# Gate and up products of a dense feed-forward by seven half-size products instead of eight

## The chip, the core and the metric

The program runs on one core of a Trainium2 chip. TensorE (PE in the profile) multiplies matrices into PSUM, VectorE (DVE) and ScalarE (ACT) work element by element, GpSimd (POOL) and SyncE (SP) here mostly start DMA transfers. Each engine runs its own instruction stream, and the streams meet at semaphores. The metric is the device time of one launch in microseconds (us); lower is better.

## What is computed

Two transformer stacks of two layers each run on one sequence of 256 tokens of 1024 values, all in float32. What matters here are three dense feed-forward blocks (both layers of the first stack, the first layer of the second), each of width 2816:

```python
gate, up = jnp.split(jnp.einsum('bsd,df->bsf', h, ffn_w_gate_up[l]), 2, axis=-1)
f = jnp.einsum('bsf,fd->bsd', jax.nn.silu(gate) * up, ffn_w_down[l])

def dense_swiglu(x, w_gate, w_up, w_down):
    return (jax.nn.silu(x @ w_gate) * (x @ w_up)) @ w_down
```

The last layer has a mixture of eight experts of width 3584 instead, which takes the time from about 1450 us to the end. The change does not touch it.

## The kernel before

**Stages.** The program is a list of stages (mixers, projections, norms, feed-forwards), and each engine walks the same list with its own code. Weights are read from memory once, in blocks of at most 2 MB, into six slots of SBUF (`slots`); SP starts the load of block n as soon as TensorE has marked block n - 6 as used. So a load follows TensorE's progress.

**One dense feed-forward.** The 2816 columns are cut into six groups: five of 512 and one of 256. A group has a gate block, an up block (1024 x 512) and a down block (512 x 1024). The tokens lie transposed in `hT`: 128 partitions x 8 chunks of the 1024 input values x 256 tokens. A *pair* is 256 columns of a group, so a group of 512 has two pairs, the last group one. A pair has two *units*, gate and up: 256 output columns x 256 tokens x 1024 inputs. The first group (`first_gate_up`) is worked in halves of 128 tokens, since the two token tiles become ready one after the other; the other five groups go through `gate_up`: 9 pairs, 18 units in each feed-forward, 54 units in the program.

**One unit before.** For each of two blocks of 128 columns, TensorE adds up eight products over the chunks k in one PSUM bank (128 x 512: two blocks x 256 tokens):

```python
last = pe.matmul(b[:, f * S:(f + 1) * S], v[:, k, (f0 + f) * P:(f0 + f + 1) * P],
                 hT[:, k, :], start=(k == 0), stop=(k == KD - 1))
```

The weights' 128 x 128 block is the operand that is loaded into the array (LDWEIGHTS), the 256 tokens are moved through it. Gate units go to the two banks `ps_a`, up units to the two banks `ps_d`. ScalarE takes silu of the gate bank into `silu`, VectorE multiplies that with the up bank into `hid` (part of the buffer `proj`).

**Order on TensorE.** Group 0 (halves), gate and up of group 1, down of group 0, gate and up of group 2, down of group 1, and so on; the downs of the last two groups come after the last gate and up, one token tile after the other. `down` (16 products of 512 moved columns for a full group) accumulates in the four banks `ps_s` and `ps_x` and waits for `hid` of its own pairs only.

Of the kernel before, what the change touches and what calls it, by code (L numbers as in the profile page):

```python
# [25 lines left out]
P = 128  # L26
D = 1024
S = 256
# [471 lines left out]
def build(nc, a, out, book, cut=None):  # L500
# [21 lines left out]
    with ExitStack() as ctx:  # L522
        def sb(name, shape, dt=F32):
            return ctx.enter_context(nc.sbuf_tensor(name, shape, dt))
# [5 lines left out]
        def sem(name):  # L530
# [19 lines left out]
        dve_order, act_order, pool_order, exped, maxed = (  # L550
            sem(n) for n in ("dve_order", "act_order", "pool_order", "exped", "maxed"))

        slots = sb("slots", [P, SLOTS, SLOT])
        X = sb("X", [P, T, D])
        N = sb("N", [P, T, D])
# [56 lines left out]
        order_s = flat[:, 3200:3456]  # L612
        earlier, every = QK[:, 0, 0, :], QK[:, 0, 1, :]
        silu = flat[:, 2048:3072].rearrange("p (b s) -> p b s", b=2)
        logits = flat[:, 3072:3088].rearrange("p (t e) -> p t e", t=T)
        route = flat[:, 3088:3200]
        NF = N[:, :, :].rearrange("p t c -> p (t c)")
        VC = NF[:, 0:1024].rearrange("p (t c) -> p t c", t=T)
        score = NF[:, 1024:1536].rearrange("p (t s) -> p t s", t=T)
        work = NF[:, 1536:2048].rearrange("p (t s) -> p t s", t=T)  # L620
        DOf = DO[:, :, :].rearrange("p t c -> p (t c)")
# [357 lines left out]
        def _(pe):  # L979
# [246 lines left out]
            def first_gate_up(group, s, stage_n):  # L1226
# [18 lines left out]
                state["pair"] += group["w"] // P // 2  # L1245
                return state["pair"] - 1

            def gate_up(group):
                gv, uv = slot(group["gate"]), slot(group["up"])
                for f0 in range(0, group["w"] // P, 2):  # L1250
                    for w, v, r in (("gate", gv, "a"), ("up", uv, "d")):
# [8 lines left out]
                group_pair = state["pair"] - 1  # L1260
                return group_pair
# [499 lines left out]
        def _(act):  # L1761
# [146 lines left out]
            def ffn(s, stage_n):  # L1908
                for t in range(T):
                    turn_tile(s, stage_n, t)  # L1910
                for group in s["groups"]:
                    for _ in range(group["w"] // P // 2):
                        b, n = bank(lane, "a")
                        act.wait_ge(*lane.of(("full", "a", n)))
                        p = state["pair"]
                        state["pair"] += 1
# [229 lines left out]
        def _(dve):  # L2146
# [609 lines left out]
            def ffn(groups):  # L2756
                for group in groups:
                    n_group = state["group"]
                    state["group"] += 1
                    dve.wait_ge(*lane.back(("down",), n_group - 2))  # L2760
                    for f0 in range(0, group["w"] // P, 2):
                        p = state["pair"]
                        state["pair"] += 1
                        dve.wait_ge(*lane.of(("silu", p)))
                        b, n = bank(lane, "d")
                        dve.wait_ge(*lane.of(("full", "d", n)))
                        dve.tensor_tensor(  # L2767
                            hid[:, n_group % 2, f0:f0 + 2, :].rearrange("p f s -> p (f s)"), silu[:, p % 2, :],
                            b[:, :], ALU.mult).then_inc(*lane.tick(d_free, ("free", "d", n), ("hidden", p)))

            for n, (kind, s) in enumerate(stages):
                lane.ring.update(ring_at[n])
# [4 lines left out]
                if kind == "lines":  # L2777
                    b, m = bank(lane, "d")
                    dve.wait_ge(*lane.of(("full", "d", m)))
                    for v in range(2):  # L2780
                        do(dve.tensor_tensor(lines[:, v, :], b[0:16, :], line_mask[:, v, :], ALU.add),
                           ("lines",), ("free", "d", m), sem=d_free)
                elif kind == "norm":
                    norm(s, n)
                elif kind == "last_norm":
                    last_norm(s)
                elif kind == "first_slots":
                    first_slots(s["steps"], s["downs"])
                elif kind == "head_norms":
                    head_norms(s)  # L2790
                elif kind == "mla_keys":
                    mla_keys()
                elif kind == "attend":
                    attend(s, n)
                elif kind == "attend_head":
                    attend(stages[n + s["ahead"]][1], n + s["ahead"], head=True)
                elif kind == "latent_norm":
                    dve.wait_ge(*lane.of(("latent",)))
                    dve.wait_ge(*lane.of(("lin", s["src"], 0, 1)))
                    c = proj[:, :, 512:640]  # L2800
                    squares(c, P, SQ[:, 0])
                    inv_root(T, stat[:, 32:34], 1.0 / P, LN_EPS)
                    for t in range(T):
                        do(dve.scalar_tensor_tensor(c[:, t, :], c[:, t, :], stat[:, t:t + 1], small[:, 0:P],
                                                    ALU.mult, ALU.mult), ("latent_normed",))
                elif kind == "index_scores":
                    do(dve.memset(score, 0.0))
                    dve.wait_ge(*lane.of(("lin", s["src"], 1, 1)))
                    do(dve.tensor_scalar(proj[:, :, 1216:1224], proj[:, :, 1216:1224], 8 ** -0.5, None, ALU.mult))
                    for h in range(8):  # L2810
                        dve.wait_ge(*lane.of(("relu", h)))
                        for t in range(T):
                            do(dve.scalar_tensor_tensor(score[:, t, :], PR[h // 2 % 2][:, h % 2, t, :],
                                                        proj[:, t, 1216 + h:1217 + h], score[:, t, :],
                                                        ALU.mult, ALU.add), ("indexed", h))
                elif kind == "select":
                    select(s)
                elif kind == "gates":
                    dve.wait_ge(*lane.of(("gate_exp",)))
                    do(dve.tensor_scalar(gate_t[:, :, :], gate_t[:, :, :], 1.0, None, ALU.add))  # L2820
                    do(dve.reciprocal(gate_t[:, :, :], gate_t[:, :, :]))
                elif kind == "compress_in":
                    compress_in()
                elif kind == "compress_hidden":
                    compress_hidden()
                elif kind == "compress_out":
                    compress_out()
                elif kind == "ended_scores":
                    ended_scores()
                elif kind == "ended_out":  # L2830
                    ended_out(n)
                elif kind == "latent_heads":
                    attend(stages[n + 1][1], n + 1, head=True)
                elif kind == "route":
                    route_tokens(s)
                elif kind == "ffn":
                    ffn(s["groups"])
# [40 lines left out]
```

## Time and profile before

| | us |
|---|---|
| median of 3 runs | 2364.01 |
| lowest and highest | 2359.44 and 2368.95 |
| the profiled execution | 2360.85 |
| its span, first to last instruction | 2359.0 |
| TensorE busy | 2260.9 |
| VectorE busy | 451.3 |
| ScalarE busy | 354.3 |

The span and the profiled execution's own time lie 1.85 us apart; the profiled execution lies 3.16 us under the median. The profile records each float32 matmul as two passes, each with a weight load and a product: `gate_up` issues 27 pairs x 16 = 432 products into `ps_a`, and line 1256 has 864 of them. A product's record lasts longer than its share of the engine, because products overlap; the distance from start to start is what one costs.

### The profile page before, as it was taken

The page shows a single profiled execution, that of the slowest core. Times are in us where ns is not written, and L with a number is a line of the kernel's source. Part 1 is how long each engine was busy: PE and PEld are TensorE (multiplying, and loading weights), DVE is VectorE, ACT ScalarE, POOL GpSimd, SP SyncE. Part 2 cuts the span into 40 slices and gives each one's busy share as a digit, 9 for nine tenths or more (in the row PEclk, how much of TensorE's full clock was granted, in tenths as well). Part 3 has the DMA queues.
Part 4 walks back from the last instruction along what each step waited for, and adds up shares of the span by engine and source line. Part 5 has one row for each costly group of instructions (what it writes and reads, how often), then busy time and mean ns, then how long its engine had stood idle before and what let it go on. Part 6 is the DMA issues. An engine that isn't in the chain of part 4 may idle for free. (4 is left out here: it accounts for less than half of the span.)

```text
span 2359.0 us, 31883 instructions
## 1 busy us (share of the span) xinstructions
PE 2260.9 (96%) x13831; PEld 1331.0 (56%) x13831; DVE 451.3 (19%) x1173; ACT 354.3 (15%) x891; POOL 108.0 (5%) x188
## 2 busy tenths in 40 slices
PE   8999999999999999999999998999899899989986
PEld 5769675687777567787758766333333233323322
DVE  3231002342000344200021534101010011101012
ACT  1330000161000123200001613110010011000000
POOL 2202000001000011000000200000000000000000
PEclk9799999999999999999998998999999999999998
DMA  9605424584444353444343434899999999999994
GB/s 305 216 17 205 166 85 163 149 196 165 150 143 138 100 199 141 152 160 143 104 149 134 149 116 160 341 368 406 407 405 409 404 409 404 409 400 409 400 409 183
DMA packets 196934, 564.32 MB, mean 239 GB/s; under 512 B 9832, under 2 KB 25384, under 8 KB 196792
## 3 DMA queue, kind: packets, MB, share of 16 engines
q1 hardware_dynamic: 187352, 536.95, 61.3%
q0 software_dynamic: 9440, 25.28, 3.7%
q8 instruction: 113, 1.85, 0.3%
q14 instruction: 29, 0.24, 0.0%
HBM read 554.60 MB, written 7.60 MB: 238 GB/s over the span
## 5 line engine op out<-in xcount | busy, mean ns | idle before, releaser
L1256 PE MATMUL ps_a<-hT,slots 128*128 128x256 f32 x864 | 190.9, 379 | 0.0
L1256 PE MATMUL ps_d<-hT,slots 128*128 128x256 f32 x864 | 190.9, 379 | 0.0
L1505 PE MATMUL ps_d<-slots,hT 128*32 128x512 f32 x1456 | 183.2, 593 | 6.9 <-DMA late<-in_moe_w_up 2.6
L1256 PEld LDWEIGHTS ps_a<-hT,slots 128*128 128x128 f32 x864 | 163.9, 190 | 27.3 <-issue 5.7
L1256 PEld LDWEIGHTS ps_d<-hT,slots 128*128 128x128 f32 x864 | 164.2, 190 | 22.3
L1505 PE MATMUL ps_d<-slots,N 128*32 128x512 f32 x1344 | 166.3, 593 | 8.1 <-DMA slots<-in_moe_w_up 3.0
L1054 PE MATMUL ps_a<-hT,slots 128*128 128x256 f32 (+1 forms) x768 | 144.3, 349 | 1.9 <-ACT hT L1791 1.5
L1054 PEld LDWEIGHTS ps_a<-hT,slots 128*128 128x128 f32 x768 | 127.4, 193 | 19.1 <-issue 5.6
L2767 DVE TENSOR_TENSOR proj<-proj,ps_d 128x512 f32<-128x512 f32 x33 | 22.7, 687 | 590.6 <-PE ps_d L1256 519.3
L2690 DVE TENSOR_TENSOR proj<-proj,ps_d 64x512 f32<-64x512 f32 (+2 forms) x32 | 22.1, 689 | 569.9 <-PE ps_d L1505 321.0
L1273 PE MATMUL ps_x<-slots,proj 128*128 128x512 f32 x264 | 121.6, 592 | 0.0
L1273 PE MATMUL ps_s<-slots,proj 128*128 128x512 f32 x264 | 121.6, 592 | 0.0
L1505 PEld LDWEIGHTS ps_d<-slots,hT 128*32 128x32 f32 x1456 | 51.9, 110 | 118.0 <-issue 114.0
L1029 PE MATMUL ps_a<-slots,hT 128*128 128x512 f32 (+5 forms) x320 | 107.1, 491 | 2.8 <-ACT hT L1791 2.8
L1505 PEld LDWEIGHTS ps_d<-slots,N 128*32 128x32 f32 x1344 | 47.1, 110 | 108.6 <-issue 103.6
L1918 ACT ACTIVATE proj<-ps_a 128x512 f32<-128x512 f32 x33 | 19.7, 597 | 537.7 <-PE ps_a L1256 511.6
L1572 PE MATMUL ps_x<-slots,PT 128*32 128x512 f32 x672 | 80.0, 621 | 16.1 <-DMA slots<-in_moe_w_down 15.3
L1989 ACT ACTIVATE PT<-ps_a 128x512 f32<-128x512 f32 x44 | 25.1, 596 | 423.6 <-PE ps_a L1594 423.5
L1553 PE MATMUL ps_x<-slots,PT 128*32 128x512 f32 x672 | 88.4, 593 | 0.0
L1029 PEld LDWEIGHTS ps_a<-slots,hT 128*128 128x128 f32 x320 | 59.5, 199 | 47.8 <-issue 45.2
L1273 PEld LDWEIGHTS ps_x<-slots,proj 128*128 128x128 f32 x264 | 50.2, 190 | 63.1 <-issue 63.1
L1273 PEld LDWEIGHTS ps_s<-slots,proj 128*128 128x128 f32 x264 | 50.2, 190 | 56.7 <-issue 56.0
(403 smaller groups left out, 2587.7 us busy)
## 6 DMA issues: line engine op xcount, KB each, us to landing
slots<-in_moe_w_gate SPq DMA_DIRECT2D x43, 2048.0 KB, 20.6
slots<-in_moe_w_down SPq DMA_DIRECT2D x42, 2048.0 KB, 20.9
slots<-in_moe_w_up SPq DMA_DIRECT2D x41, 2048.0 KB, 23.0
slots<-in_ffn_w_gate_up SPq DMA_DIRECT2D x20, 2048.0 KB, 8.0
late<-in_moe_w_up SPq DMA_DIRECT2D x15, 2048.0 KB, 23.0
late<-in_moe_w_down SPq DMA_DIRECT2D x14, 2048.0 KB, 20.4
late<-in_moe_w_gate SPq DMA_DIRECT2D x13, 2048.0 KB, 23.9
slots<-in_ffn_w_down SPq DMA_DIRECT2D x10, 2048.0 KB, 8.1
```

Source lines behind the costliest of these rows:

```text
L1029: last = pe.matmul(b[:, 0:c], lhs[:, k, t * P:(t + 1) * P], v[:, k, :], start=(k == 0), stop=(k == s["k"] - 1))
L1054: last = pe.matmul(b[:, f * S + tokens.start:f * S + tokens.stop], v[:, k, part["c"] + P * f:part["c"] + P * f + P], lhs[:, k, tokens], st ...
L1256: last = pe.matmul(b[:, f * S:(f + 1) * S], v[:, k, (f0 + f) * P:(f0 + f + 1) * P], hT[:, k, :], start=(k == 0), stop=(k == KD - 1))
L1273: last = pe.matmul(b[:, :], hid[:, n_group % 2, f, t * P:(t + 1) * P], v[:, f, half * 512:(half + 1) * 512], start=start, stop=stop)
L1505: last = pe.matmul(b[TILE * j:TILE * j + TILE, :], x[:, k, TILE * c:TILE * c + TILE], views[w][:, k % deep, 512 * h:512 * h + 512], start= ...
L1553: last = pe.matmul(b0[TILE * j:TILE * j + TILE, :], mine(f + o, c), v[:, f + o, 512 * half:512 * half + 512], start=(first and o == 0), st ...
L1572: last = pe.matmul(b[TILE * j:TILE * j + TILE, :], hid_a[:, f, o:o + TILE], v[:, f, 512 * half:512 * half + 512], start=(at == 0 and f == ...
L1918: act.activation(silu[:, p % 2, :], b[:, :], ACT.Silu).then_inc(*lane.tick(a_free, ("free", "a", n), ("silu", p)))
L1989: act.activation(dst.rearrange("p f s -> p (f s)"), b[:, :], ACT.Copy).then_inc(*lane.tick(a_free, ("free", "a", n), *[("hid_turned", i) f ...
L2690: post(dve.tensor_tensor(hidden[low:high, half, :], gated[low:high, half, :], b[low:high, :], ALU.mult), *marks, *([("free", r, n)] if m = ...
L2767: dve.tensor_tensor(hid[:, n_group % 2, f0:f0 + 2, :].rearrange("p f s -> p (f s)"), silu[:, p % 2, :], b[:, :], ALU.mult).then_inc(*lane. ...
```

## The change

All groups but the first go by Strassen's scheme (in the variant with common sums). A unit is seen as a 2 x 2 block product: inputs in two halves (chunks 0 to 3 and 4 to 7), columns in two blocks of 128 (f0, f0 + 1), tokens in two tiles of 128. Instead of eight half-size products there are seven, each of four chunks, of 128 columns x 128 tokens.

- **TensorE** (`gate_up`, `seven_products`): a unit takes two banks of its ring. The first gets three products, the second four; each product adds up four chunks. Before a unit it waits for `weights_summed`.
- **VectorE before the products**: once in a feed-forward `sum_tokens` makes four sums of token quarters (128 x 512 each) into the buffers `PR`; for each unit `sum_weights` makes four sums of weight quarters (128 x 512 each), three into a buffer for gate (`PT`) or up (part of `proj`), one in place in the weight slot. There is one such buffer each for gate and up. Sums for group 1 are made ahead of the first multiply of group 0.
- **After the products**: ScalarE copies one 128 x 128 product to SBUF; VectorE's `join` adds them up in four instructions (256, 256, 256 and 128 values per partition) into SBUF (`N`). ScalarE then takes silu from there, VectorE multiplies from there.
- **VectorE's order in the loop**: join gate of pair p, sums of gate weights of p + 1, join up of p, sums of up weights of p + 1, multiply p.

```diff
             def gate_up(group):
-                        b, n = bank(lane, r)
-                        pe.wait_ge(*emptied(lane, r, n))
-                        for f in range(2):
-                            for k in range(KD):
-                                last = pe.matmul(b[:, f * S:(f + 1) * S], v[:, k, (f0 + f) * P:(f0 + f + 1) * P],
-                                                 hT[:, k, :], start=(k == 0), stop=(k == KD - 1))
-                        last.then_inc(*lane.tick(filled[r], ("full", r, n), ("used", group[w])))
+                        v, (t2, t3, t4) = views[w], weight_sums[w]
+                        b11, t1 = (v[:, 0:4, P * f:P * f + P] for f in (f0, f0 + 1))
+                        b21, b22 = (v[:, 4:8, P * f:P * f + P] for f in (f0, f0 + 1))
+                        b, n = bank(lane, r)
+                        pe.wait_ge(*emptied(lane, r, n))
+                        pe.wait_ge(*lane.of(("weights_summed", w, state["pair"])))
+                        seven_products([(0, b11, a11), (1, b21, a12), (2, t2, s2)], b, n, r)
+                        b, n = bank(lane, r)
+                        pe.wait_ge(*emptied(lane, r, n))
+                        seven_products([(2, t3, s3), (1, t1, s1), (0, t4, a22), (3, b22, s4)], b, n, r, ("used", group[w]))
...
+            def seven_products(products, b, n, r, *keys):
+                for at, lhs, rhs in products:
+                    for k in range(4):
+                        last = pe.matmul(b[:, P * at:P * at + P], lhs[:, k, :], rhs[:, k, :], start=(k == 0), stop=(k == 3))
+                last.then_inc(*lane.tick(filled[r], ("full", r, n), *keys))
...
+            def sum_weights(w, group, f0, p):
+                dve.wait_ge(*lane.of(("weights", group[w])))
+                do(dve.tensor_tensor(t3, b22, b12, ALU.subtract), sem=weights_summed)
+                do(dve.tensor_tensor(b12, b12, b11, ALU.subtract), sem=weights_summed)
+                do(dve.tensor_tensor(t2, b22, b12, ALU.subtract), sem=weights_summed)
+                do(dve.tensor_tensor(t4, b21, t2, ALU.subtract), ("weights_summed", w, p), sem=weights_summed)
...
+            def join(w, r, p):
+                dve.wait_ge(*lane.of(("first", w, p)))
+                do(dve.tensor_tensor(ahead_of[w].rearrange("p (m s) -> p m s", m=2)[:, :, 0:P],
+                                     one.unsqueeze(1).broadcast_to([P, 2, P]),
+                                     first[:, P:3 * P].rearrange("p (m s) -> p m s", m=2), ALU.add), ("free", r, n), sem=joined)
+                dve.wait_ge(*lane.of(("full", r, n)))
+                do(dve.tensor_tensor(u[:, 1:3], u[:, 0:1].broadcast_to([P, 2, P]), m[:, 1:3], ALU.add), sem=joined)
+                do(dve.tensor_tensor(c[:, :, 1], u[:, 2:3].broadcast_to([P, 2, P]), m[:, 0:2], ALU.add), sem=joined)
+                do(dve.tensor_tensor(c[:, 1, 0], u[:, 1], m[:, 3], ALU.add), ("free", r, n), ("joined", w, p), sem=joined)
```

TensorE, first feed-forward, from the end of group 0 on, before: one pair is a gate unit and an up unit of 16 products with 256 moved columns each; after two pairs the down of group 0 follows.

```order
L1240 MATMUL ps_d<-hT,slots 128x128 x16
L1256 MATMUL ps_a<-hT,slots 128x256 [waits a_free,slot_landed0,slot_landed5]
L1256 MATMUL ps_a<-hT,slots 128x256 x15
L1256 MATMUL ps_d<-hT,slots 128x256 [waits d_free]
L1256 MATMUL ps_d<-hT,slots 128x256 x15
```

The same place after (`PR` and `late` hold token sums, `PT` and `proj` weight sums); the rows are one gate unit and the head of its up unit.

```order
L1251 MATMUL ps_d<-hT,slots 128x128 x16
L1263 MATMUL ps_a<-hT,slots 128x128 [waits a_free,weights_summed,slot_landed0,slot_landed5]
L1263 MATMUL ps_a<-hT,slots 128x128 x7
L1263 MATMUL ps_a<-PR,PT 128x128 x4
L1263 MATMUL ps_a<-late,PT 128x128 [waits a_free]
L1263 MATMUL ps_a<-late,PT 128x128 x3
L1263 MATMUL ps_a<-PR,slots 128x128 x4
L1263 MATMUL ps_a<-hT,PT 128x128 x4
L1263 MATMUL ps_a<-late,slots 128x128 x4
L1263 MATMUL ps_d<-hT,slots 128x128 [waits weights_summed,d_free]
L1263 MATMUL ps_d<-hT,slots 128x128 x7
```

A unit of 16 products of 256 columns became 28 products of 128 columns, with a wait for VectorE at its head and a wait for its second bank after 12 products.

VectorE in the same feed-forward, before: one multiply for each pair is all that it does there.

```order
L2767 TENSOR_TENSOR proj<-proj,ps_d 128x512 [waits d_full,a_free,x_landed0]
L2767 TENSOR_TENSOR proj<-proj,ps_d 128x512 [waits d_full,a_free]
L2767 TENSOR_TENSOR proj<-proj,ps_d 128x512 [waits d_full,a_free,down_done]
L2767 TENSOR_TENSOR proj<-proj,ps_d 128x512 [waits d_full,a_free]
L2767 TENSOR_TENSOR proj<-proj,ps_d 128x512 [waits d_full,a_free,down_done]
```

VectorE after, for the first pair of group 1: the join of gate, the sums for the next pair's gate, and the join of up.

```order
L2820 TENSOR_TENSOR N<-N,ps_a 128x2x128 [waits act_order]
L2826 TENSOR_TENSOR N<-N,ps_a 128x256 [waits a_full,joined]
L2827 TENSOR_TENSOR N<-N,ps_a 128x2x128 [waits joined]
L2828 TENSOR_TENSOR N<-N,ps_a 128x128 [waits joined]
L2809 TENSOR_TENSOR PT<-slots 128x512 [waits slot_landed5,joined]
L2810 TENSOR_TENSOR slots<-slots 128x4x128 [waits weights_summed]
L2811 TENSOR_TENSOR PT<-slots 128x512 [waits weights_summed]
L2812 TENSOR_TENSOR PT<-slots,PT 128x512 [waits weights_summed]
L2820 TENSOR_TENSOR N<-proj,ps_d 128x2x128 [waits act_order,weights_summed]
L2826 TENSOR_TENSOR N<-N,ps_d 128x256 [waits d_full,joined]
L2827 TENSOR_TENSOR N<-N,ps_d 128x2x128 [waits joined]
L2828 TENSOR_TENSOR N<-N,ps_d 128x128 [waits joined]
```

Behind these follow four sums for the next pair's up and the multiply of this pair; where one instruction stood for a pair, 17 stand now, and the sums for the next gate unit stand behind the last three joins of this one.

## Rows read from the trace of the kernel before

**Rows 1.** The page: busy time by engine, then the span in 40 slices.

```profile
PE 2260.9 (96%) x13831; PEld 1331.0 (56%) x13831; DVE 451.3 (19%) x1173; ACT 354.3 (15%) x891; POOL 108.0 (5%) x188
...
PE   8999999999999999999999998999899899989986
...
PEclk9799999999999999999998998999999999999998
DMA  9605424584444353444343434899999999999994
```

**Rows 2.** Windows: first group, gate and up, down, experts; busy time of each engine.

```profile
core 0: us, PE busy (x) PEld busy (x) DVE busy (x) ACT busy (x) POOL busy (x), PEclk, DMA share, GB/s
176.80:206.86 30.06, 29.79 (x264) 29.57 (x265) 6.58 (x12) 4.29 (x8) 15.26 (x21) 1.00 0.64 213
206.86:234.49 27.63, 27.63 (x130) 24.33 (x129) 1.37 (x2) 1.19 (x2) 0.00 (x0) 1.00 0.53 200
234.49:248.23 13.74, 13.74 (x34) 6.08 (x33) 0.69 (x1) 0.00 (x0) 0.00 (x0) 1.00 0.47 165
1450.00:2350.00 900.00, 845.77 (x7199) 288.26 (x7197) 108.03 (x216) 83.57 (x148) 0.53 (x1) 0.97 0.97 384
```

**Rows 3.** Timeline of PE, first feed-forward: group 0 second half, group 1, down.

```profile
start us, us, engine line op out<-in xcount [idle before <-releaser]
192.47 3.84 PE L1240 MATMUL ps_a<-hT,slots 128*128 128x128 f32 x32 [0.25 <-ACT hT L1791]
196.14 3.74 PE L1240 MATMUL ps_d<-hT,slots 128*128 128x128 f32 x32
199.72 3.74 PE L1240 MATMUL ps_a<-hT,slots 128*128 128x128 f32 x32
203.29 3.74 PE L1240 MATMUL ps_d<-hT,slots 128*128 128x128 f32 x32
206.86 7.07 PE L1256 MATMUL ps_a<-hT,slots 128*128 128x256 f32 x32
213.77 7.07 PE L1256 MATMUL ps_d<-hT,slots 128*128 128x256 f32 x32
...
234.49 1.88 PE L1273 MATMUL ps_s<-slots,proj 128*128 128x512 f32 x4
...
248.23 2.11 PE L1256 MATMUL ps_a<-hT,slots 128*128 128x256 f32 x9
```

**Rows 4.** Instructions of line 1240 and line 1256: duration in ns, least, median, greatest.

```profile
L1240 PEld LDWEIGHTS ps_a<-hT,slots x384: 186/192/192, 176.8 to 1019.7; 128*128 128x128 f32 x192
L1256 PE MATMUL ps_a<-hT,slots x864: 379/379/382, 206.9 to 1195.7; 128*128 128x256 f32 x173
```

**Rows 5.** Line 1239: what a wait beyond an instruction's own becomes on PE's queue.

```profile
L1239 PEldq EVENT_SEMAPHORE  x3: 51/51/51, 176.7 to 993.4; - x3
```

**Rows 6.** Groups by line and shape on DVE and ACT: count, busy us, mean ns.

```profile
L2767 DVE TENSOR_TENSOR proj<-proj,ps_d 128x512 f32<-128x512 f32 x33 | 22.7, 687 | 590.6 <-PE ps_d L1256 519.3 <-PE ps_d L1240 71.3
L2209 DVE TENSOR_TENSOR X<-X,N 128x1024 f32<-128x1024 f32 x8 | 9.8, 1224 | 0.3
L2390 DVE TENSOR_TENSOR hT<-hT 128x256 f32<-128x256 f32 x8 | 3.4, 425 | 0.3
L2343 DVE TENSOR_TENSOR late<-late,N 128x128 f32<-128x128 f32 x6 | 1.7, 285 | 0.0
L1861 ACT ACTIVATE late<-ps_s,negmax 128x128 f32<-128x128 f32 x24 | 9.3, 387 | 0.2
```

**Rows 7.** Timeline of DVE and ACT in the first feed-forward.

```profile
191.82 1.08 ACT L1791 ACTIVATE hT<-ps_s 128x512 f32<-128x512 f32 x2 [9.83 <-PE ps_s L1007]
...
234.76 0.69 DVE L2767 TENSOR_TENSOR proj<-proj,ps_d 128x512 f32<-128x512 f32 x1 [13.10 <-PE ps_d L1256]
...
400.05 1.23 DVE L2209 TENSOR_TENSOR X<-X,N 128x1024 f32<-128x1024 f32 x1
401.31 1.22 DVE L2211 CUSTOM_DVE_ANT_0 N<-X 128x1024 f32<-128x1024 f32 x1
```

**Rows 8.** What SP waits for before it starts loads, then one load and its landing time.

```profile
SPq L790 <- PE ps_a L1256: 263.6, 15, 20.3
...
SPq L790 <- PE ps_d L1505: 207.4, 51, 18.0
...
slots<-in_ffn_w_gate_up SPq DMA_DIRECT2D x20, 2048.0 KB, 8.0
```

**Rows 9.** Timeline of SP: the loads of groups 3 (gate, up) and 2 (down).

```profile
227.78 7.27 SPq L790 DMA_DIRECT2D slots<-in_ffn_w_gate_up  x2
248.42 0.37 SPq L790 DMA_DIRECT2D slots<-in_ffn_w_down  x1
```

More of the change, by code:

```diff
@@ L614, in build @@
         silu = flat[:, 2048:3072].rearrange("p (b s) -> p b s", b=2)
+        token_sums = [buf.rearrange("p a t s -> p (a t s)")[:, 512 * i:512 * i + 512].rearrange("p (k s) -> p k s", k=4)
+                      for buf in (PR[0][:, :, :, :], PR[1]) for i in range(2)]
+        weight_sums = {w: [buf[:, 512 * i:512 * i + 512].rearrange("p (k c) -> p k c", k=4) for i in range(3)]
+                       for w, buf in (("gate", PT[:, :, :, :, :].rearrange("p a j k n -> p (a j k n)")[:, 0:1536]),
+                                      ("up", flat[:, 3072:4608]))}
         logits = flat[:, 3072:3088].rearrange("p (t e) -> p t e", t=T)
@@ L618, in build @@
         VC = NF[:, 0:1024].rearrange("p (t c) -> p t c", t=T)
+        whole = {"gate": NF[:, 0:512], "up": NF[:, 512:1024]}
+        partial = NF[:, 1024:1408].rearrange("p (m s) -> p m s", m=3)
+        ahead_of = {"gate": NF[:, 0:2048], "up": NF[:, 512:1536]}
+        first_product = {"gate": NF[:, 1408:1536], "up": flat[:, 4608:4736]}
         score = NF[:, 1024:1536].rearrange("p (t s) -> p t s", t=T)
@@ L1910, in ffn @@
                     turn_tile(s, stage_n, t)
-                for group in s["groups"]:
+                for g, group in enumerate(s["groups"]):
                     for _ in range(group["w"] // P // 2):
+                        p = state["pair"]
+                        state["pair"] += 1
+                        if not g:
+                            bank(lane, "d")
+                        if g:
+                            for w, r in (("gate", "a"), ("up", "d")):
+                                b, n = bank(lane, r)
+                                bank(lane, r)
+                                act.wait_ge(*lane.of(("full", r, n)))
+                                act.activation(first_product[w], b[:, 0:P], ACT.Copy).then_inc(*lane.tick(act_order, ("first", w, p)))
+                            act.wait_ge(*lane.of(("joined", "gate", p)))
+                            act.wait_ge(*lane.back(("hidden",), p - 2))
+                            act.activation(silu[:, p % 2, :], whole["gate"], ACT.Silu).then_inc(*lane.tick(act_order, ("silu", p)))
+                            continue
                         b, n = bank(lane, "a")
                         act.wait_ge(*lane.of(("full", "a", n)))
-                        p = state["pair"]
-                        state["pair"] += 1
                         act.wait_ge(*lane.back(("hidden",), p - 2))
@@ L2754, in expert, with sum_tokens @@
                             *lane.tick(emptying[r], ("free", r, n)))
[L2756 to L2759, printed above, removed]
-                    dve.wait_ge(*lane.back(("down",), n_group - 2))
[L2761 to L2769, printed above, removed]
+            def sum_tokens(stage_n):
+                for t in range(T):
+                    dve.wait_ge(*lane.of(("hT", stage_n, t, 4)))
+                a11, a12 = hT[:, 0:4, 0:P], hT[:, 4:8, 0:P]
+                a21, a22 = hT[:, 0:4, P:S], hT[:, 4:8, P:S]
+                s1, s2, s3, s4 = token_sums
+                do(dve.tensor_tensor(s1, a21, a22, ALU.add), sem=tokens_summed)
+                do(dve.tensor_tensor(s2, s1, a11, ALU.subtract), sem=tokens_summed)
+                do(dve.tensor_tensor(s3, a11, a21, ALU.subtract), sem=tokens_summed)
+                do(dve.tensor_tensor(s4, a12, s2, ALU.subtract), sem=tokens_summed)
@@ new lines, in ffn @@
+            def ffn(groups, stage_n):
+                sum_tokens(stage_n)
+                units = [(group, f0) for group in groups for f0 in range(0, group["w"] // P, 2)]
+                lead, p0 = groups[0]["w"] // P // 2, state["pair"]
+                for w in ("gate", "up"):
+                    sum_weights(w, *units[lead], p0 + lead)
+                for _ in range(lead):
+                    bank(lane, "a")
+                for i, (group, f0) in enumerate(units):
+                    p = p0 + i
+                    if f0 == 0:
+                        n_group = state["group"]
+                        state["group"] += 1
+                    target = hid[:, n_group % 2, f0:f0 + 2, :].rearrange("p f s -> p (f s)")
+                    if i >= lead:
+                        for w, r in (("gate", "a"), ("up", "d")):
+                            join(w, r, p)
+                            if i + 1 < len(units):
+                                sum_weights(w, *units[i + 1], p + 1)
+                    dve.wait_ge(*lane.back(("down",), n_group - 2))
+                    dve.wait_ge(*lane.of(("silu", p)))
+                    if i >= lead:
+                        dve.tensor_tensor(target, silu[:, p % 2, :], whole["up"], ALU.mult).then_inc(
+                            *lane.tick(dve_order, ("hidden", p)))
+                        continue
+                    b, n = bank(lane, "d")
+                    dve.wait_ge(*lane.of(("full", "d", n)))
+                    dve.tensor_tensor(target, silu[:, p % 2, :], b[:, :], ALU.mult).then_inc(
+                        *lane.tick(d_free, ("free", "d", n), ("hidden", p)))
+                state["pair"] += len(units)
@@ L2836, in _ @@
                 elif kind == "ffn":
-                    ffn(s["groups"])
+                    ffn(s["groups"], n)
                 elif kind == "experts":
```

18 lines of the change are left out of this document (14 added, 4 removed).

## The prediction

> **What bounds the kernel now.** I read the page's busy line and slices first [rows 1]. TensorE is busy 96% of the span, VectorE 19%, ScalarE 15%. The DMA row falls into two parts: some four tenths up to slice 23, nine tenths after it. So TensorE's work sets the time before the experts, and transfers may set it there. Next the windows [rows 2]: in the gate and up window of group 1 TensorE is busy for all of 27.63 us, VectorE for 1.37 us, DMA for 0.53 of the time; in the experts DMA is at 0.97. The feed-forwards are therefore TensorE's, without a gap to fill. Then the timeline [rows 3], for what one product costs. Its second number is the length of the records of a group; the first numbers, the starts, give the rate. Last come VectorE's groups and gaps [rows 6, 7], because it gets the new work, and SP's waits [rows 8, 9], because a gain on TensorE counts only if the loads behind it move as well.
>
> **The change part by part: TensorE.** Four units of group 1 run from 206.86 to 234.49 us [rows 3], so a unit takes 27.63 / 4 = 6.908 us. It has 16 products of two passes each (864 records for 432 products, [rows 4]); a pass of 256 columns thus costs 6.908 / 32 = 215.9 ns. A new unit has 28 products of 128 columns, 56 passes. The columns moved fall to 7/8 (56 x 128 against 32 x 256), but the weight loads rise from 32 to 56. What a pass of 128 columns with a fresh 128 x 128 load costs needn't be guessed: group 0 consists of such passes. From 196.14 to 206.86 us there are 96, without a gap [rows 3]: 111.7 ns each, only 3.7 ns above half a 256-column pass. A load's record lasts 192 ns [rows 4], yet starts follow at 111.7 ns, so loads overlap their neighbours; the load rows fill 29.57 of 30.06 us there [rows 2], so hardly any room is left. New unit: 56 x 111.7 = 6.253 us. Gain: 0.654 us a unit, in 54 units **35.3 us**. The granted clock was 1.00 (the 2.4 GHz level) in both windows [rows 2], and the new stream is as dense, so I leave it there.
>
> The Trainium skill speaks against this step: "TensorE: Matmul & The Clock Gate", section "Back-to-back issue gap", gives a stream of load and product pairs some 81 ns per product at 128 columns, where the columns alone would take about 56, that is 1.46 times as much. Applied as a ratio, an estimate from that page, a pass here would cost 158 ns and a unit 8.8 us, and the kernel would end near 2468 us. The trace has 1.03 times instead [rows 3], and that decides.
>
> **Waits on TensorE.** A unit's head now has one wait more, and in its middle one for the second bank. A wait beyond an instruction's own became an instruction of 51 ns on PE's queue [rows 5]. Down's first product waits for more than one thing too (four in the first feed-forward), and yet starts 27.63 us after the units, in step with 32 passes each [rows 3]: no cost there, but behind slow passes. In a stream of 111.7 ns passes the queue has less time to hide it. Bounds: 0 and 54 x 0.051 = 2.8 us; a further wait can't make a pass quicker, so nothing below nought. Neither row is nearer; I take the middle, 1.4 us.
>
> **VectorE, sums.** No row shows a sum of 512 values out of SBUF alone. An addition of 512 with one operand in PSUM takes 687 ns, one of 1024 within SBUF 1224 ns [rows 6], which halved is 612. I take 687, since the fixed part of a short instruction is in it; the far end is 1224. From start to start 30 ns come on top (400.05 to 401.31 against 1.224, [rows 7]). A unit's four sums: 4 x 0.717 = 2.87 us. The joins: 256 values take 425 ns, 128 take 285 ns [rows 6]; 3 x 0.455 + 0.315 = 1.68 us. Together 4.55 us a unit beside 6.25 us of TensorE, and over 54 units, with the 12 token sums, some 254 us more busy time on VectorE, all of it off the path as long as each deadline holds.
>
> **The deadline.** There is one weight-sum buffer each for gate and up, so the sums of the next gate unit may begin only when this one has ended, and so for up. From a unit's end: 0.27 us until VectorE starts (234.76 against 234.49, [rows 3, 7]), the last three joins 1.23 us, the sums 2.87 us: ready 4.37 us after. TensorE spends 6.25 us on the other unit meanwhile: **1.9 us to spare**. Behind the last pair of a group a down of 13.74 us lies between as well [rows 2]. The join's first instruction needs ScalarE's copy of 128 values (nearest row 387 ns, [rows 6]) of a bank filled 3.5 us before the unit ends, so it is done by then. What is queued behind these waits on VectorE is the multiply; down needs it only after the next group's units.
>
> **Start and end of a feed-forward.** VectorE can begin its token sums when `hT` is copied, at 192.90 us [rows 7]. Four sums and the four for gate end at 198.6; TensorE wants them at 206.86. The first multiply waits behind all 12, to 201.5 us; its bank is wanted at 213. At the end the last pair is ready 0.27 + 1.23 + 0.72 = 2.2 us after its unit, while TensorE first does half of a down, 13.74 / 2 = 6.9 us [rows 2]. Nothing is exposed; if the cover failed, this costs at most a few us in each of three feed-forwards.
>
> **Loads.** VectorE asks for a group's weights about 20 us sooner than TensorE did. Group 3's gate and up were issued from 227.78 us on [rows 9] and land after some 8 us [rows 8]; VectorE asks for them in the second pair of group 2, after 260 us. SP waits for TensorE's marks in the feed-forwards and in the experts alike [rows 8], so the stages behind, the DMA-bound one too, start earlier by the whole gain.
>
> **The sum.** Against the profiled execution: 2360.85 - 35.3 + 1.4 = 2326.9 us. That execution lies 3.2 us under the median of the runs, so **2330 us**.
>
> **The rivals.**
>
> *VectorE late* (slower). For: the sums are strided over four chunks, read two SBUF operands, and depend on each other; such a shape isn't in the trace. Against: additions within SBUF cost what their length says [rows 6]. Only the second pair of each two-pair group is exposed, 24 units (2 units x 4 groups x 3). Were all the instructions twice as long, a unit's sums would be ready after 0.27 + 2 x 4.10 = 8.5 us, 2.2 us late: 24 x 2.2 = 53 us lost on top of the forecast, 2330 + 53 = **2383 us**. It decides from 1.80 times the rows' durations on (0.27 + 1.80 x 4.10 = 7.65 us, 1.4 us late, x 24 = 34 us). Chance 0.06.
>
> *Weight loads not hidden* (slower). If loads from the sum buffers don't overlap as group 0's do, a pass costs up to its load's 192 ns [rows 4]: 56 x 0.192 = 10.75 us a unit, 3.84 us more, 207 us in all: 2571 us. It decides from 6.908 / 56 = 123.4 ns a pass on, which makes the margin thin: 10% above group 0's. Against: same form, same stream, 96 passes in a row at 111.7. Chance 0.04. By the page above this rival would end at 2468.
>
> *Half of it lost*. Each wait that VectorE or a bank releases late by 0.1 to 0.3 us over 54 units takes 5 to 16 us: 2335 to 2346 us. Chance 0.09.
>
> *No change*. Some 0.45 us or more of stall a unit, or a later stage that waits for something else than TensorE. Against the latter: SP's waits [rows 8]. Around 2358 us. Chance 0.05. That fewer products are issued than seven, or more, the order of the instructions excludes.
>
> **How the numbers follow.** The forecast has 0.76, at 2330 us; with its own bounds (0 or 2.8 us of waits, and runs that spread by 5 us either way) 2323 to 2337. To hold 8 in 10 the range takes in most of the half-lost case: 2321 to 2346. Faster by over 0.5% (about what a measurement of this kernel can tell from no change, 12 us): 0.76 + 0.09 = 0.85; within it 0.05; slower 0.06 + 0.04 = 0.10.
>
> **What would show it.** In the profile after: units 6.25 us apart from start to start, 56 passes each of 111 to 112 ns, load rows nearly without a gap; group 1 with its down in 38.8 us instead of 41.4; VectorE's sums at 0.69 us and its busy time near 705 us; no idle time of TensorE ahead of the units put down to VectorE; the experts as long as before, only earlier. Wrong would be: TensorE waiting for the sums at the second pair's units, passes above 123 ns, or sums well over 1 us.

## The result and the profile after

| | before | after |
|---|---|---|
| median, us | 2363.82 (4 runs) | 2327.25 (4 runs) |
| lowest and highest, us | 2359.44 and 2368.95 | 2323.76 and 2330.76 |
| the profiled execution, us | 2360.85 | 2323.76 |
| its span, us | 2359.0 | 2322.0 |

The ratio of the times is 0.9845, 95% interval 0.9829 to 0.9861: the changed kernel is faster by 36.6 us of the medians. The forecast was 2330 us, with a range of 2321 to 2346.

The page's busy line of the kernel after, to be held against [rows 1]:

```profile
PE 2226.2 (96%) x15127; PEld 1338.5 (58%) x15127; DVE 694.9 (30%) x1617; ACT 367.2 (16%) x945; POOL 108.5 (5%) x188
```

TensorE is busy 34.7 us less, VectorE 243.6 us more, and the span fell by 37.0 us. VectorE's work has thus left no mark that can be seen from this far. Next the windows of the kernel after. The columns are those of [rows 2]; the first line is group 1's gate and up, the second the down of group 0, the third both together, the last a stretch of the experts.

```profile
206.06:231.07 25.01, 25.01 (x226) 25.01 (x225) 14.66 (x27) 2.15 (x6) 0.00 (x0) 1.00 0.56 211
231.07:244.81 13.74, 13.74 (x35) 6.09 (x34) 4.59 (x8) 0.00 (x0) 0.00 (x0) 1.00 0.52 181
206.06:244.81 38.75, 38.75 (x259) 31.10 (x258) 19.25 (x35) 2.15 (x6) 0.00 (x0) 1.00 0.55 200
1413.00:2313.00 900.00, 846.61 (x7197) 287.49 (x7195) 107.75 (x215) 83.62 (x148) 0.53 (x1) 0.97 0.98 384
```

Gate and up of a group take 25.01 us where they took 27.63, the down 13.74 as before. TensorE is still busy for the whole window, and so now is its weight load (25.01 of 25.01). VectorE is busy for 14.66 us of it instead of 1.37, and the clock stays at 1.00. A 900 us stretch of the experts holds nearly the same work at the same DMA share, begun 37 us earlier. The experts' first product shows the same shift, 37.5 us, before (first line) and after (second line):

```profile
1471.78 8.79 PE L1505 MATMUL ps_d<-slots,hT 128*32 128x512 f32 x80 [0.50 <-ACT hT L1926]
1434.29 13.94 PE L1528 MATMUL ps_d<-slots,hT 128*32 128x512 f32 x128 [0.50 <-ACT hT L1961]
```

(The two counts and lengths differ because the listings end at different times.)

The timeline of TensorE after shows the same group from start to start; the columns are those of [rows 3]. The lines left out are the other products of each unit.

```profile
206.06 1.95 PE L1263 MATMUL ps_a<-hT,slots 128*128 128x128 f32 x16
207.84 1.06 PE L1263 MATMUL ps_a<-PR,PT 128*128 128x128 f32 x8
...
211.42 1.06 PE L1263 MATMUL ps_a<-late,slots 128*128 128x128 f32 x8
212.31 1.95 PE L1263 MATMUL ps_d<-hT,slots 128*128 128x128 f32 x16
...
218.56 1.95 PE L1263 MATMUL ps_a<-hT,slots 128*128 128x128 f32 x16
...
224.82 1.95 PE L1263 MATMUL ps_d<-hT,slots 128*128 128x128 f32 x16
...
231.07 1.88 PE L1296 MATMUL ps_s<-slots,proj 128*128 128x512 f32 x4
```

Units start at 206.06, 212.31, 218.56 and 224.82 us, and the down at 231.07: 25.01 / 4 = 6.25 us a unit, 56 passes of 111.7 ns. No line of these four units carries an idle time in brackets, the lines left out included, so TensorE waited neither for sums nor for a bank.

How the sums fit beside this is seen on VectorE, from the end of the gate unit of the first pair (212.31 us) on:

```profile
212.58 0.42 DVE L2826 TENSOR_TENSOR N<-N,ps_a 128x256 f32<-128x256 f32 x1 [2.91 <-PE ps_a L1263]
213.04 0.42 DVE L2827 TENSOR_TENSOR N<-N,ps_a 128x256 f32<-128x256 f32 x1
213.49 0.29 DVE L2828 TENSOR_TENSOR N<-N,ps_a 128x128 f32<-128x128 f32 x1
213.81 0.69 DVE L2809 TENSOR_TENSOR PT<-slots 128x512 f32<-128x512 f32 x1
...
215.99 0.69 DVE L2812 TENSOR_TENSOR PT<-slots,PT 128x512 f32<-128x512 f32 x1
```

VectorE starts 0.27 us after the unit's end, and the last of the four sums ends at 215.99 + 0.69 = 216.68 us, 4.37 us after it. TensorE wants them at 218.56.

**Where the time went.** I measured the first and the third feed-forward from the first product of group 0 to the first transpose of the norm behind it. The second is measured from the transposes between the two token halves of group 0 on, in both kernels, so it lacks the first half of group 0, which the change doesn't touch. These are windows of the kernel before (the first three lines) and of the kernel after (the last three), one line for each feed-forward, with the same columns:

```profile
176.82:406.72 229.90, 229.65 (x1017) 172.39 (x1017) 21.63 (x37) 11.34 (x20) 15.26 (x21) 1.00 0.45 158
571.36:786.90 215.54, 215.29 (x891) 158.03 (x890) 12.93 (x21) 10.42 (x16) 0.00 (x0) 1.00 0.40 138
993.47:1223.38 229.91, 229.66 (x1017) 172.40 (x1017) 17.98 (x28) 10.97 (x18) 9.76 (x19) 1.00 0.42 143
```

```profile
176.01:394.15 218.14, 217.89 (x1448) 175.52 (x1449) 103.75 (x185) 15.63 (x38) 15.69 (x21) 1.00 0.48 167
558.71:762.49 203.78, 203.53 (x1323) 161.16 (x1322) 93.09 (x169) 14.83 (x34) 0.00 (x0) 1.00 0.42 147
969.30:1187.45 218.15, 217.90 (x1449) 175.52 (x1449) 98.16 (x176) 15.26 (x36) 9.75 (x19) 1.00 0.43 151
```

Each lost 11.76 us (229.90 - 218.14, and so on), that is 18 units x 0.653 us; three times that is 35.3 us. The remaining 1.7 us of the two spans lie outside the feed-forwards, where the change does nothing: 0.8 us ahead of the first one, 1.6 us between the third and the experts, and the rest with the other sign. They are within what two executions of one kernel differ by.

### The profile page after: what moved, and what is told of

Read it like the earlier page. It is cut to its first block, busy times and chain, and to the rows that moved or that the text cites. A ratio compares the mean times of both kernels' runs of the same rounds, so it can differ in the third digit from the quotient of the medians.

```text
span 2322.0 us, 35165 instructions
## 1 busy us (share of the span) xinstructions
PE 2226.2 (96%) x15127; PEld 1338.5 (58%) x15127; DVE 694.9 (30%) x1617; ACT 367.2 (16%) x945; POOL 108.5 (5%) x188
## 4 chain that ended last, share of the span: by engine, by line
PE 85%; DMA 10%; ACT 2%; POOL 1%; DVE 1%; SPq 1%; issue 1%; DVEq 0%; ACTq 0%
PE ps_d L1528 14%; PE ps_d L1263 7%; PE ps_a L1263 7%; PE ps_a L1065 6%; PE ps_s L1296 5%; PE ps_x L1296 5%; PE ps_a L1040 5%; PE ps_x L1576 4%; PE ps_s L1528 4%; PE ps_x L1177 3%; DMA late<-in_moe_w_up 3%; PE ps_s L1110 3%; PE ps_x L1110 3%; PE ps_x L1595 2%; DMA slots<-in_moe_w_up 2%; PE ps_x L1582 2%
## 5 line engine op out<-in xcount | busy, mean ns | idle before, releaser
L1065 PEld LDWEIGHTS ps_a<-hT,slots 128*128 128x128 f32 x768 | 127.4, 193 | 19.2 <-issue 5.6
L1528 PE MATMUL ps_d<-late,N 128*32 128x512 f32 x512 | 74.6, 593 | 2.6 <-DMA slots<-in_moe_w_up 1.5
L1110 PE MATMUL ps_s<-slots,hT 128*128 128x512 f32 x160 | 72.2, 596 | 2.7 <-ACT hT L1825 2.7
L1177 PE MATMUL ps_x<-proj,PT 128*128 128x64 f32 (+1 forms) x560 | 71.6, 284 | 0.0
L1177 PEld LDWEIGHTS ps_x<-proj,PT 128*128 128x128 f32 x560 | 70.5, 204 | 0.0
L1110 PE MATMUL ps_x<-slots,hT 128*128 128x512 f32 x160 | 69.6, 592 | 0.0
L2003 ACT ACTIVATE proj<-ps_d 32x512 f32<-32x512 f32 (+3 forms) x56 | 33.1, 591 | 222.4 <-PE ps_d L1528 221.8
```

Source lines behind the costliest of these rows:

```text
L1065: last = pe.matmul(b[:, f * S + tokens.start:f * S + tokens.stop], v[:, k, part["c"] + P * f:part["c"] + P * f + P], lhs[:, k, tokens], st ...
L1110: last = pe.matmul(b[:, :], hT[:, k, t * P:(t + 1) * P], v[:, k, :], start=(k == ks[0]), stop=(k == ks[-1]))
L1177: last = pe.matmul(b[:, o:o + dv], PT[:, u % 2, j, turned_at[kc, t], :], named[name][:, kc, c:c + dv], start=(kc == kcs[0]), stop=(kc == k ...
L1528: last = pe.matmul(b[TILE * j:TILE * j + TILE, :], x[:, k, TILE * c:TILE * c + TILE], views[w][:, k % deep, 512 * h:512 * h + 512], start= ...
L2003: act.activation(dst, src, ACT.Silu).then_inc(*lane.tick(a_free if frees else act_order, ("gate_silu", q), *([("free", "d", n)] if frees e ...
```

## The experiments

The theory: TensorE's passes are the whole of it, seven eighths of the columns at nearly the same price per column, and VectorE's sums lie in TensorE's shadow with under 2 us to spare. Against it stood that the new pass costs more than counted, that the sums or the waits cost something which another gain hides, and that the spare time is no more than a number on paper.

### The shape alone: eight products in halves

The kernel before, with each unit's 256 tokens moved in two halves of 128. All eight half-size products remain, and nothing is summed.

```diff
-                            for k in range(KD):
-                                last = pe.matmul(b[:, f * S:(f + 1) * S], v[:, k, (f0 + f) * P:(f0 + f + 1) * P],
-                                                 hT[:, k, :], start=(k == 0), stop=(k == KD - 1))
+                            for t in range(T):
+                                for k in range(KD):
+                                    last = pe.matmul(b[:, f * S + t * P:f * S + t * P + P],
+                                                     v[:, k, (f0 + f) * P:(f0 + f + 1) * P],
+                                                     hT[:, k, t * P:t * P + P], start=(k == 0), stop=(k == KD - 1))
```

> The kernel before, with each unit cut into eight half-size products (four blocks of 128 columns x 128 tokens, each over eight chunks) instead of products of 256 moved columns: the shape of the changed kernel without its seventh saved. My theory (a pass of 128 columns costs 111.7 ns wherever it stands, and only the number of passes counts): a unit takes 64 x 111.7 = 7.15 us instead of 6.91, 54 units lose 12.9 us, so 12 to 14 us above the kernel before. Rival (the gain of the change comes from its shape or from smaller products, not from their number): at or below the time before. Rival (a pass of 128 columns is dearer in some other place than group 0): over 14 us above it.

Measured: 2380.28 us median, against 2364.62 of the kernel before beside it; ratio 1.0053, interval 1.0035 to 1.0070, so 12.5 us slower (2364.62 x 0.0053). The two medians lie 15.7 us apart, which taken alone would be past the 14 us of the second rival. The window of the first feed-forward decides between them:

```profile
179.26:413.48 234.22, 233.97 (x1592) 191.59 (x1593) 21.64 (x37) 11.34 (x20) 15.25 (x21) 1.00 0.45 155
```

It takes 4.32 us more than before (234.22 - 229.90), in three feed-forwards 13.0 us, so a pass of 128 columns isn't dearer here than in group 0. The timeline of TensorE in this kernel:

```profile
209.31 7.31 PE L1257 MATMUL ps_a<-hT,slots 128*128 128x128 f32 x64
216.45 7.31 PE L1257 MATMUL ps_d<-hT,slots 128*128 128x128 f32 x64
223.60 7.31 PE L1257 MATMUL ps_a<-hT,slots 128*128 128x128 f32 x64
230.75 7.31 PE L1257 MATMUL ps_d<-hT,slots 128*128 128x128 f32 x64
237.89 1.88 PE L1275 MATMUL ps_s<-slots,proj 128*128 128x512 f32 x4
```

A unit takes (237.89 - 209.31) / 4 = 7.145 us, which is 64 passes of 111.6 ns. So the gain of 0.654 us a unit falls into two parts: the smaller blocks cost 7.145 - 6.908 = 0.24 us, and the eighth product that isn't made gives back 8 x 111.7 = 0.89 us.

### No sums at all

The kernel after, without the token sums, the weight sums and TensorE's wait for them; each product takes a plain quarter in place of the sum. Its values are thus others, and send the tokens to other experts. That makes the last stage, and the whole time, something else (4905.75 us), so only the feed-forwards compare.

```diff
-                s1, s2, s3, s4 = token_sums
+                s1, s2, s3, s4 = hT[:, 0:4, P:S], hT[:, 4:8, 0:P], hT[:, 4:8, P:S], hT[:, 0:4, 0:P]
...
+                        t2, t3, t4 = b11, b21, b22
...
-                        pe.wait_ge(*lane.of(("weights_summed", w, state["pair"])))
...
             def sum_weights(w, group, f0, p):
-                dve.wait_ge(*lane.of(("weights", group[w])))
+                return
...
-                sum_tokens(stage_n)
```

> The changed kernel without the sums of weights and of tokens and without TensorE's wait for them: the seven products take plain quarters of weights and tokens instead, so the block products are not those of the layer. The joins stay. My theory (VectorE's sums lie wholly beside TensorE's work): within 3 us of the changed kernel, 2327 us, units still 6.25 us apart. Rival (the sums or the waits for them cost TensorE something): faster by 5 us or more.

The total missed what was expected (within 3 us of the changed kernel), since I had not thought of the tokens' way to the experts. The window of the first feed-forward of this kernel, whole as above:

```profile
176.20:394.34 218.14, 217.89 (x1448) 175.59 (x1449) 49.57 (x109) 15.62 (x38) 15.27 (x21) 1.00 0.48 167
```

It takes 218.14 us, as with the sums, though VectorE is busy 49.57 us in it instead of 103.75. The third feed-forward takes 218.14 us too, against 218.15. Sums and waits for them cost TensorE nothing that a hundredth of a microsecond shows.

### How much room there is: two, three and four more sums

The kernel after, with the sum into `t2` made again two, three or four times, the result unchanged. The kernel with three more was made after the other two had been measured, and its forecast draws on them. For two more:

```diff
                 do(dve.tensor_tensor(t2, b22, b12, ALU.subtract), sem=weights_summed)
+                do(dve.tensor_tensor(t2, b22, b12, ALU.subtract), sem=weights_summed)
+                do(dve.tensor_tensor(t2, b22, b12, ALU.subtract), sem=weights_summed)
                 do(dve.tensor_tensor(t4, b21, t2, ALU.subtract), ("weights_summed", w, p), sem=weights_summed)
```

> The changed kernel with the third sum of each unit's weights made three times instead of once, two instructions of 0.72 us more before the sums are ready. My theory (1.9 us to spare between the sums and the unit that needs them): ready 5.8 us after the last unit of the same kind instead of 4.4, still ahead of 6.25, so the time stays within 3 us of the changed kernel. Rival (less is to spare than that, or VectorE's load counts by itself): 54 x 1.43 us at worst, 77 us slower; anything over 5 us speaks for it.

> As the kernels with two and with four more, with three instructions of 0.72 us more for each unit. With two more TensorE never waited, with four it waited at 24 units, about 1.2 us each counted from start to start, of which 0.15 us lies between the end of the last sum and TensorE's start. My theory: sums ready 4.37 + 2.18 + 0.15 = 6.70 us after the last unit of the same kind, 0.45 us past the 6.25: 24 units x 0.45 to 0.55 us, so 11 to 13 us above the changed kernel, 2338 to 2341. Rival (two or four more differ for another reason than the deadline, for instance VectorE's total load): half way between the two, some 15 us or more above, or none.

> As the kernel with two more, but four instructions of 0.72 us more for each unit. My theory: ready 7.2 us after, about 1.0 us late for the second pair's gate unit of each two-pair group and 1.2 us late for its up unit; 12 such groups, so some 26 us (20 to 32) above the changed kernel, and TensorE idle only there, with VectorE as what ends the wait. Rival (the down hides it all, or the lateness adds up over all 54 units): no change, or some 50 us and more.

| sums for a unit | median, us | ratio to before, interval | first feed-forward, us | waits of TensorE for sums |
|---|---|---|---|---|
| 4 (after) | 2327.25 | 0.9845 (0.9829 to 0.9861) | 218.14 | none |
| 6 | 2328.16 | 0.9834 (0.9804 to 0.9863) | 218.14 | none |
| 7 | 2340.83 | 0.9911 (0.9888 to 0.9934) | 222.27 | 24 |
| 8 | 2359.40 | 0.9976 (0.9962 to 0.9990) | 228.10 | 24 |

Two more sums, 1.45 us a unit, cost nothing that shows. Three more cost 4.13 us in the first feed-forward, four more 9.96. By the medians three cost 13.6 us, where 11 to 13 were expected, and four 32.2 us, where 26 (20 to 32) were; by the feed-forwards alone it is 12.4 and 29.8 us. The first waits on TensorE's timeline, of the kernel with three more sums (first fence) and with four more (second and third fence; the second has all of TensorE's waits for sums, us in total, times and longest, and the last sum on VectorE):

```profile
217.43 1.06 PE L1263 MATMUL ps_d<-late,slots 128*128 128x128 f32 x8
218.77 2.02 PE L1263 MATMUL ps_a<-hT,slots 128*128 128x128 f32 x16 [0.28 <-DVE PT L2815]
...
225.53 2.02 PE L1263 MATMUL ps_d<-hT,slots 128*128 128x128 f32 x16 [0.28 <-DVE proj L2815]
```

```profile
PE ps_a L1263 <- DVE PT L2816: 12.1, 12, 1.0
PE ps_d L1263 <- DVE proj L2816: 12.1, 12, 1.0
...
217.63 0.69 DVE L2816 TENSOR_TENSOR PT<-slots,PT 128x512 f32<-128x512 f32 x1
```

```profile
216.40 1.06 PE L1263 MATMUL ps_d<-late,slots 128*128 128x128 f32 x8
218.47 2.02 PE L1263 MATMUL ps_a<-hT,slots 128*128 128x128 f32 x16 [1.01 <-DVE PT L2816]
...
225.97 2.02 PE L1263 MATMUL ps_d<-hT,slots 128*128 128x128 f32 x16 [1.01 <-DVE proj L2816]
```

With four more sums the last one ends at 217.63 + 0.69 = 218.32 us, and TensorE's first pass follows at 218.47: 0.15 us go by between the two engines. It was due at 216.40 + 8 x 0.1117 = 217.29, so it is 1.18 us late; the bracket shows less (1.01), because records of products reach past their share of the engine. The first 16 passes after such a stop also take 0.07 us longer (220.33 - 218.47 = 1.86 against 1.79). Together 1.25 us, on 24 units 30 us; the three feed-forwards lost 29.8 (9.96, 9.94 and 9.93). These are the units of the second pair of a two-pair group, 8 in each feed-forward, that the prediction named as the exposed ones.

### Half the columns

The kernel after, with only 64 of the 128 columns of each product moved, so that half of each product is left out; other values go to other experts here too, and only the feed-forwards compare.

```diff
-                        last = pe.matmul(b[:, P * at:P * at + P], lhs[:, k, :], rhs[:, k, :], start=(k == 0), stop=(k == 3))
+                        last = pe.matmul(b[:, P * at:P * at + 64], lhs[:, k, :], rhs[:, k, 0:64], start=(k == 0), stop=(k == 3))
```

> The changed kernel with only 64 of the 128 columns moved in each of the seven products; the other half of each product is left out, so the layer's values are wrong, tokens go to other experts, and only the feed-forward stretch can be compared. My theory (at 128 columns a pass already costs about what its weight load costs, 107 ns or so, and that floor is what holds it 3.7 ns above half a 256-column pass): passes 105 to 110 ns apart, units 5.9 to 6.2 us instead of 6.25. Rival (the columns set the pass): about 56 ns a pass, units near 3.2 us, with TensorE then waiting for VectorE's sums (4.4 us).

The timeline of TensorE in this kernel:

```profile
204.09 1.95 PE L1263 MATMUL ps_a<-hT,slots 128*128 128x64 f32 x16
205.87 1.06 PE L1263 MATMUL ps_a<-PR,PT 128*128 128x64 f32 x8
...
210.34 1.95 PE L1263 MATMUL ps_d<-hT,slots 128*128 128x64 f32 x16
...
216.59 1.94 PE L1296 MATMUL ps_s<-slots,proj 128*128 128x512 f32 x4
```

Units of 6.25 us (210.34 - 204.09, 216.59 - 210.34), passes of 111.7 ns: not a nanosecond was saved by half the columns. I had expected a little to come off (units of 5.9 to 6.2 us), and that was wrong: the floor is the whole 111.7 ns. With a fresh 128 x 128 load, 64 columns are no quicker than 128. The load rows fill the whole window (25.01 of 25.01 us above), so the load is the likely bound, but that is not shown; what a smaller load would take was not tried. The Trainium skill, "TensorE: Matmul & The Clock Gate", section "LDWEIGHTS (loading the stationary operand)", lets a load's time go with its columns alone, 128 / 1.2 = 107 ns here, an estimate from that page; the trace's spacing of 111.7 ns agrees to 5%, while a load's own record lasts 192 ns. At 256 columns the pass takes 215.9 ns [rows 3], nearly twice as long. Half of that, 108 ns, is an estimate of what 128 columns alone would take; the floor lies only 4 ns above it. So from 256 columns to 128 a pass falls in price nearly with its columns, and from 128 to 64 not at all; the seven products of 128 columns stand just above that edge.

## Why the prediction was right, and where it was off

- **Price and number of passes: right.** 56 x 111.7 ns, 6.253 us forecast, 6.25 measured, in all 54 units. Group 0 of the kernel before already was the new stream, and it held also with operands from the sum buffers: the loads of `PR,PT` passes last 192 ns as those of [rows 4] do. This line of the kernel after gives count, then least, median and greatest duration in ns:

```profile
L1263 PEld LDWEIGHTS ps_a<-PR,PT x216: 192/192/192, 207.7 to 1156.8; 128*128 128x128 f32 x108
```

- **Waits on TensorE: mis-sized, 1.4 us taken, 0 measured.** The wait did become an instruction of its own before each of the 54 units, as [rows 5] had it for three others, and its price is the lower end of the bounds, 0 (15 more such instructions stand at line 1277, for a bank):

```profile
L1278 PEldq EVENT_SEMAPHORE  x54: 51/51/51, 204.2 to 1158.6; - x54
```

  Units are no further apart than in the kernel without the wait for sums. TensorE's queue runs ahead of its passes also where these take only 111.7 ns: the first of them starts at 204.2 us, 1.8 us ahead of its unit.

- **VectorE's durations: right.** A sum takes 0.69 us (0.687 taken, from a row with one operand in PSUM), joins 0.42 and 0.29. That a sum is strided, reads two SBUF operands and hangs on the sum before it costs nothing that can be seen. Count and durations in ns, kernel after:

```profile
L2810 DVE TENSOR_TENSOR slots<-slots x54: 691/691/694, 196.8 to 1142.8; 128x512 f32<-128x512 f32 x54
L2826 DVE TENSOR_TENSOR N<-N,ps_a x27: 420/422/422, 212.6 to 1160.9; 128x256 f32<-128x256 f32 x27
L1945 ACT ACTIVATE N<-ps_a x27: 277/278/278, 208.9 to 1157.2; 128x128 f32<-128x128 f32 x27
```

  VectorE's busy time is 694.9 us where near 705 was forecast, and ScalarE's copy 278 ns where the nearest row had 387. Neither is on the path, since TensorE waited for neither.

- **The deadline: right in its working, 0.15 us too generous.** Sums are ready 4.37 us after the unit, to the hundredth as worked out. The 1.9 us to spare leave out the way from VectorE's end to TensorE's first pass; it is 6.25 - 4.37 - 0.15 = 1.73 us. Two more sums (1.45 us) fit, three (2.18 us) are 0.45 us too late, as measured.

- **VectorE late, the rival: it did not come true, and where I made it true it was priced nearly right.** To cost anything the sums had to grow by 1.73 us a unit, six tenths of their 2.87, and they were as the rows said. With twice as many sums the 24 units named as exposed were 1.18 us late each and lost 1.25 us each, 30 us in the feed-forwards, most of the gain of 35.3; the prediction had counted the lateness alone, without the 0.07 us after a stop. It had put the point from which the rival decides at 1.4 us of delay, and 1.18 us leaves a kernel at 0.9976 of before.

- **Start and end of a feed-forward: hidden as said, the start longer than said.** The first multiply starts 10.7 us after the first token sum (202.91 against 192.23 us), where 8.6 were worked out (201.5 against 192.90), because two sums took over twice their time (below). Its bank is wanted at 212.31. At the end the last pair is ready 2.19 us after its unit, as worked out, and TensorE goes on with the down without a gap.

- **Loads: right.** SP, whose rows follow, now starts group 3's gate and up at 225.01 instead of 227.78 us [rows 9] (three units' gain, 1.96 us, and 0.8 us from ahead of the feed-forward), and what it waits for are TensorE's marks as in [rows 8]: 238.1 us on 15 waits instead of 263.6. VectorE nowhere waited for a load into the slots. That the experts come earlier by the whole gain, their first products above show.

```profile
225.01 6.62 SPq L801 DMA_DIRECT2D slots<-in_ffn_w_gate_up  x2
...
SPq L801 <- PE ps_a L1263: 238.1, 15, 18.4
```

Without the waits the sum is 2360.85 - 35.3 = 2325.6 instead of 2326.9 us; the profiled execution took 2323.76, and the last 1.8 us are no part of the change. The median lies 2.75 us below the forecast. One ratio in the paragraph that the prediction sets against its own price of a pass is slightly off: 81 to 56 is 1.45 and not 1.46, so 158 ns and 2468 us should be some 156 ns and 2463 us. No forecast or chance hangs on it.

## What to carry to other kernels

An algorithm with fewer products pays only as far as the smaller product isn't dearer on this engine: look for a stretch of the old kernel that already runs the new shape, and multiply its start-to-start time by the new count. Here smaller blocks took back 0.24 of 0.89 us a unit, and as half the columns again save nothing, a second such step with half the tokens would make 7/4 times as many passes at the same price (an estimate from that row; not tried). Work put on another engine cost nothing here until its last result, plus the way between the engines, missed the deadline; beyond that point each exposed unit paid the full lateness. So the room is counted against one unit's deadline (1.73 us here), and not against a busy share, be it 30% of the span or 59% of the gate and up window (14.66 of 25.01 us).

## What the runs showed that I had not expected

Two of the sums at the first feed-forward's start took 1.64 and 1.71 us instead of 0.69. The timelines of VectorE (first fence) and GpSimd (second fence), kernel after:

```profile
193.68 1.64 DVE L2800 TENSOR_TENSOR late<-hT 128x512 f32<-128x512 f32 x1
...
198.26 0.69 DVE L2812 TENSOR_TENSOR PT<-slots,PT 128x512 f32<-128x512 f32 x1
198.98 1.71 DVE L2809 TENSOR_TENSOR proj<-slots 128x512 f32<-128x512 f32 x1
```

```profile
187.60 1.26 POOL L977 TENSOR_TENSOR late<-late 128x512 f32<-128x512 f32 x1 [6.08 <-DMA late<-table_scratch]
...
193.10 1.67 POOL L977 TENSOR_TENSOR late<-late 128x512 f32<-128x512 f32 x1 [1.83 <-DMA late<-table_scratch]
...
198.88 1.27 POOL L977 TENSOR_TENSOR late<-late 128x512 f32<-128x512 f32 x1 [1.68 <-DMA late<-table_scratch]
```

Each ran into an addition of GpSimd's that had begun before it, and ended 0.55 and 0.54 us after GpSimd's end (193.10 + 1.67 = 194.77 and 195.32; 200.15 and 200.69), as if it had hardly begun until then. One of GpSimd's additions, begun while VectorE was in a sum, took 1.67 us instead of 1.26. The Trainium skill, "SBUF — State Buffer", section "Who interferes with whom", says that a VectorE instruction with two inputs in SBUF contends with a GpSimd instruction that reads SBUF; these rows agree, and no run here took GpSimd's additions away. It cost nothing: the gate sums ended at 198.95 us, 7.1 us before TensorE wanted them (206.06), and the up sums 9.4 us before. In the middle of a feed-forward, where none occurred, one delay of 0.95 to 1.02 us would still fit into the 1.73 us, but two in one unit would not.
